# Stationary operands of the 512-column one-pass products: rounded part and rest stored apart, or element by element side by side

## The reference, cut to what matters

```python
def swiglu(h, w_gate, w_up, w_down):
    return (jax.nn.silu(h @ w_gate) * (h @ w_up)) @ w_down

for e in range(N_EXPERTS):                       # moe_swiglu
    y = swiglu(t, w_gate[e], w_up[e], w_down[e])
    out = out + combine[:, e:e + 1] * y.astype(jnp.float32)

def squared_relu_mlp(n, w1, w2):
    return jnp.square(jax.nn.relu(n @ w1)) @ w2
```

## Time and profile before

| what | value |
|---|---|
| three executions | 2759.27, 2763.17, 2770.59 us; median 2763.17 us |
| profiled execution, first to last instruction (span) | 2767.1 us |
| TensorE: matmuls (PE), weight loads (PEld) | 2704.7 us (98%), 2291.4 us (83%) |
| VectorE (DVE), ScalarE (ACT), GpSimd (POOL) | 1978.5 us (72%), 1665.1 us (60%), 86.5 us (3%) |
| HBM read, written | 697.28 MB, 18.87 MB: 259 GB/s over the span |
| mean granted TensorE clock | 0.990 |

### The profile page before, as it was taken

How to read it: one execution, slowest core, us unless ns; L and a number is a source line. 1 busy time by engine, 2 the same in 40 slices (tenths; PEclk the granted TensorE clock), 3 DMA queues, 4 the chain that set the end, 5 groups by cost and what they waited for, 6 DMA issues and landing times. The chain is left out here.

```text
span 2767.1 us, 38903 instructions
## 1 busy us (share of the span) xinstructions
PE 2704.7 (98%) x15424; PEld 2291.4 (83%) x15424; DVE 1978.5 (72%) x2069; ACT 1665.1 (60%) x1965; POOL 86.5 (3%) x86
## 2 busy tenths in 40 slices
PE   8999999999999999999999999999999999999998
PEld 5878999788988888888888888889768998867897
DVE  4756655586779998989899898986655555474555
ACT  3575444558467777777777777766445445354544
POOL 1000100110001000000000000011000000000000
PEclk8999999999999999999999999999999999999999
DMA  9847854865579999999999999986424544414452
GB/s 346 299 139 273 321 203 146 278 226 198 172 289 385 393 377 378 377 374 379 380 374 375 381 373 376 378 276 194 142 92 146 189 183 136 170 62 153 183 190 77
DMA packets 317754, 718.08 MB, mean 260 GB/s; under 512 B 7990, under 2 KB 26916, under 8 KB 317620
## 3 DMA queue, kind: packets, MB, share of 16 engines
q1 hardware_dynamic: 311488, 697.99, 69.5%
q0 software_dynamic: 5520, 18.02, 2.0%
q10 hardware_dynamic: 612, 0.18, 0.0%
HBM read 697.28 MB, written 18.87 MB: 259 GB/s over the span
## 5 line engine op out<-in xcount | busy, mean ns | idle before, releaser
L2775 DVE TENSOR_TENSOR ring_rest<-ring,weights_hi 128x2048 fp32r<-128x2048 f32 x270 | 607.5, 2284 | 9.7 <-ACT weights_hi L2100 7.3
L2100 ACT ACTIVATE weights_hi<-ring 128x2048 fp32r<-128x2048 f32 x270 | 516.6, 1916 | 131.9 <-PE ps L1833 75.7
L1831 PE MATMUL ps<-weights_hi,xg_hi 128*128 128x512 f32 x1008 | 400.9, 398 | 0.7 <-DVE xg_lo L2775 0.7
L1833 PE MATMUL ps<-weights_hi,xg_lo 128*128 128x512 f32 x1008 | 395.0, 392 | 0.0
L1832 PE MATMUL ps<-ring_rest,xg_hi 128*128 128x512 f32 x792 | 310.2, 392 | 0.0
L2100 ACT ACTIVATE arena<-ps 128x512 f32<-128x512 f32 (+6 forms) x307 | 157.3, 529 | 220.0 <-PE ps L1833 54.1
L1852 PE MATMUL ps<-weights_hi,hidden_split_moe 128*128 128x512 f32 x1008 | 284.1, 393 | 1.3 <-DVE hidden_split_moe L2775 1.1
L2775 DVE TENSOR_TENSOR w_split<-ring,w_split 128x1024 fp32r<-128x1024 f32 x128 | 150.9, 1221 | 154.5 <-ACT w_split L2100 154.5
L2775 DVE TENSOR_TENSOR ring_rest<-ring,mix_hi 128x2048 fp32r<-128x2048 f32 (+2 forms) x76 | 173.4, 2284 | 117.2 <-ACT mix_hi L2100 116.7
L2775 DVE TENSOR_TENSOR late_rest<-arena,weights_hi 128x2048 fp32r<-128x2048 f32 x108 | 244.5, 2286 | 5.3 <-ACT weights_hi L2100 4.3
L2100 ACT ACTIVATE weights_hi<-arena 128x2048 fp32r<-128x2048 f32 x108 | 207.0, 1917 | 62.3 <-PE ps L1833 32.5
(11 more groups left out here) (310 smaller groups left out, 5289.5 us busy)
## 6 DMA issues: line engine op xcount, KB each, us to landing
ring<-in_moe_w_gate_dram SPq DMA_DIRECT2D x54, 2048.0 KB, 10.1
ring<-in_moe_w_up_dram SPq DMA_DIRECT2D x45, 2048.0 KB, 10.1
ring<-in_moe_w_down_dram SPq DMA_DIRECT2D x36, 2048.0 KB, 9.2
ring<-in_mlp_w_dram SPq DMA_DIRECT2D x32, 2048.0 KB, 8.8
arena<-in_moe_w_down_dram SPq DMA_DIRECT2D x27, 2048.0 KB, 9.9
ring<-in_w_mod_dram SPq DMA_DIRECT2D x48, 1024.0 KB, 8.8
ring<-in_w_in_dram SPq DMA_DIRECT2D x48, 1024.0 KB, 6.2
arena<-in_moe_w_up_dram SPq DMA_DIRECT2D x18, 2048.0 KB, 10.4
```

Of the source, the lines that this page charges most:

```text
L1831: pe.matmul(b, xg_hi[:, k, :], hi[:, i, :], start=(k == 0), stop=False)
L1833: mm = pe.matmul(b, xg_lo[:, k, :], hi[:, i, :], start=False, stop=(k == KD - 1))
L2100: return act.activation(o, i, func, **kw)
L2775: return dve.tensor_tensor(o, a, b, op)
```

## The change

Each of the stationary tiles gets the part (rounded, rest) as its innermost dimension instead of an outer one. Element i of the rounded part and element i of the rest are then neighbours; a weight load reads 128 elements that are two elements (8 bytes) apart, and the ACT and DVE instructions that write a part write every second element. The sizes, the start addresses of the tiles, the instructions, their order and their waits stay as they are.

```diff
@@ -737,7 +737,7 @@
 
 
         expert = Region(xc_at, arena_cols - xc_at)
-        hidden_split_moe = rounded("hidden_split_moe", free_at + 2 * HALF_LINE, 2, 512)
+        hidden_split_moe = rounded("hidden_split_moe", free_at + 2 * HALF_LINE, 512, 2)
         xn_moe = expert.cut(TT, D)
         rows_moe = xn_moe[:, 0]
         to_slots = Region(rope1_at, TT * P).cut(TT, P)
@@ -761,8 +761,9 @@
         ring_rest = nc.alloc_sbuf_tensor_at("ring_rest", [P, RING_A, SLOT], F32R,
                                             offset=ring_offset)
         late_rest = rounded("late_rest", late_at, 2, SLOT)
-        xg_hi, xg_lo = rounded("xg_hi", TT * D, KD, P), rounded("xg_lo", TT * D + KD * P, KD, P)
-        xg = Region(TT * D + KD * P, KD * P).cut(KD, P)
+        xg_pairs = rounded("xg_pairs", TT * D, KD, P, 2)
+        xg_hi, xg_lo = xg_pairs[:, :, :, 0], xg_pairs[:, :, :, 1]
+        xg = Region(TT * D, 2 * KD * P).cut(KD, P, 2)[:, :, :, 1]
         before_me, all_ones = (Region(y_at + i * P, P).cut(P) for i in range(2))
         gain_row = Region(TT * D, D).cut(D)
         rpp = Region(y_at + 2 * TT * P, 512)
@@ -829,13 +830,13 @@
         hi_early_2 = rounded("hi_early_2", lru_at + 2 * TT * D, 2048)
         oT_hi = rounded("oT_hi", cross_at + 7744 + HALF_LINE, KD, T)
         hi_late_2 = rounded("hi_late_2", cross_at + 10240 + 2 * HALF_LINE, 2048)
-        hidden_split = rounded("hidden_split", cross_at + 8192 + 4 * HALF_LINE, 2, 4, 512)
+        hidden_split = rounded("hidden_split", cross_at + 8192 + 4 * HALF_LINE, 4, 512, 2)
 
         w_split_ffn = {"in": [rounded("w_in_ffn_0", lru_at + SLOT + HALF_LINE, 2, 2048), rounded("w_in_ffn_1", sg_at, 2, 2048)],
                        "out": [rounded("w_out_ffn_0", lru_at + SLOT, 2, 2048),
                                rounded("w_out_ffn_1", sg_at + 3 * HALF_LINE, 2, 2048)]}
         hT_hi_ffn = rounded("hT_hi_ffn", lru_at + TT * D, KD, T)
-        hidden_split_ffn = rounded("hidden_split_ffn", qT_at + 3 * HALF_LINE, 2, 4, T)
+        hidden_split_ffn = rounded("hidden_split_ffn", qT_at + 3 * HALF_LINE, 4, T, 2)
         setup2 = Region(pipe_at + 2816, 1280)
         posk_i, posq_i = setup2.cut(T).bitcast(I32), setup2.cut(TT).bitcast(I32)
         gain_row2 = Region(pipe_at + 2048, D).cut(D)
@@ -1751,7 +1752,7 @@
 
                             def out_part(t, c, m, q):
                                 sw, sx = parts[q]
-                                return pe.matmul(acc(t, c), hidden_split_ffn[:, sx, (2 * j + m) % 4, t * P:(t + 1) * P],
+                                return pe.matmul(acc(t, c), hidden_split_ffn[:, (2 * j + m) % 4, t * P:(t + 1) * P, sx],
                                                  w[:, sw, m, c * 512:(c + 1) * 512],
                                                  start=(j == 0 and m == 0 and q == 0),
                                                  stop=(j == FT // 2 - 1 and m == 1 and q == 2))
@@ -1849,7 +1850,7 @@
                         at = (2 * half + m) * P
                         for q, (w, sx) in enumerate([(hi, 0), (lo, 0), (hi, 1)]):
                             for c in range(2):
-                                mm = pe.matmul(acc(0, c), hidden_split_moe[:, sx, at:at + P],
+                                mm = pe.matmul(acc(0, c), hidden_split_moe[:, at:at + P, sx],
                                                w[:, m, c * 512:(c + 1) * 512],
                                                start=(g == 0 and half == 0 and m == 0 and q == 0),
                                                stop=(g == GROUPS - 1 and half == 1 and m == 1 and q == 2))
@@ -2058,7 +2059,7 @@
 
                         def out_part(t, c, m, q):
                             sw, sx = parts[q]
-                            return pe.matmul(acc(t, c), hidden_split[:, sx, j % 4, m * T + t * P:m * T + (t + 1) * P],
+                            return pe.matmul(acc(t, c), hidden_split[:, j % 4, m * T + t * P:m * T + (t + 1) * P, sx],
                                              w[:, sw, m, c * 512:(c + 1) * 512],
                                              start=(j == 0 and m == 0 and q == 0),
                                              stop=(j == n2 - 1 and m == 1 and q == 2))
@@ -2464,7 +2465,7 @@
                     act.wait_ge(emptied["dve"], plan.nth["ffn", j])
                     if j >= 4:
                         act.wait_ge(pe_done, value["ffn_out", (j - 4) // 2])
-                    f(hidden_split_ffn[:, 0, j % 4], hg[:, j % 4], ACT.Copy).then_inc(sem("ffn_hidden_rounded"), 1)
+                    f(hidden_split_ffn[:, j % 4, :, 0], hg[:, j % 4], ACT.Copy).then_inc(sem("ffn_hidden_rounded"), 1)
 
                 if l == 0:
                     round_weights(0)
@@ -2536,7 +2537,7 @@
                 else:
                     act.wait_ge(pe_done, step_at(lambda i: ("moe_down", i, GROUPS - 2), e, 1))
                     act.wait_ge(sem("hidden_moe_ready"), of_turn_at(GROUPS, GROUPS + 1, e, 1))
-                f(hidden_split_moe[:, 0, half * 256:half * 256 + 256], acc(1, 1)[:, half * 256:half * 256 + 256],
+                f(hidden_split_moe[:, half * 256:half * 256 + 256, 0], acc(1, 1)[:, half * 256:half * 256 + 256],
                   ACT.Copy).then_inc(sem("hidden_moe_rounded"), 1)
 
             def expert_head(e):
@@ -2553,7 +2554,7 @@
                             round_weights_of(p + HI_BUFFERS, e)
                     elif kind == "turn":
                         act.wait_ge(pe_done, step_at(lambda i: ("moe_T", i, at[0]), e))
-                        f(hidden_split_moe[:, 0, :], acc(1, 1), ACT.Copy).then_inc(sem("hidden_moe_rounded"), 1)
+                        f(hidden_split_moe[:, :, 0], acc(1, 1), ACT.Copy).then_inc(sem("hidden_moe_rounded"), 1)
                     else:
                         act.wait_ge(pe_done, step_at(lambda i: ("back", i), e))
                         f(to_tokens, acc(1, 0)[:, 0:T], ACT.Copy, accum_out=slot_weight)\
@@ -2732,7 +2733,7 @@
                     act.wait_ge(sem("squared"), n2 * l + j + 1)
                     if j >= 4:
                         act.wait_ge(pe_done, value["mlp_down", l, j - 4])
-                    f(hidden_split[:, 0, j % 4], squared[:, j % 2], ACT.Copy)\
+                    f(hidden_split[:, j % 4, :, 0], squared[:, j % 2], ACT.Copy)\
                         .then_inc(sem("hidden_rounded"), 1)
 
                 n2 = FF2 // P // 2
@@ -3197,7 +3198,7 @@
 
                 def rest_of_hidden(j):
                     dve.wait_ge(sem("ffn_hidden_rounded"), j + 1)
-                    tt(hidden_split_ffn[:, 1, j % 4], hg[:, j % 4], hidden_split_ffn[:, 0, j % 4].bitcast(F32),
+                    tt(hidden_split_ffn[:, j % 4, :, 1], hg[:, j % 4], hidden_split_ffn[:, j % 4, :, 0].bitcast(F32),
                        ALU.subtract).then_inc(sem("ffn_hidden_split_ready"), 1)
 
                 if l == 0:
@@ -3381,7 +3382,7 @@
             def rest_of_hidden(nth, a, z, e, back=0):
 
                 dve.wait_ge(sem("hidden_moe_rounded"), of_turn_at(nth, GROUPS + 1, e, back))
-                tt(hidden_split_moe[:, 1, a:z], acc(1, 1)[:, a:z], hidden_split_moe[:, 0, a:z].bitcast(F32),
+                tt(hidden_split_moe[:, a:z, 1], acc(1, 1)[:, a:z], hidden_split_moe[:, a:z, 0].bitcast(F32),
                    ALU.subtract).then_inc(sem("hidden_moe_ready"), 1)
 
             def outputs_taken(e):
@@ -3643,7 +3644,7 @@
 
                 def rest_of_hidden(j):
                     dve.wait_ge(sem("hidden_rounded"), n2 * l + j + 1)
-                    tt(hidden_split[:, 1, j % 4], squared[:, j % 2], hidden_split[:, 0, j % 4].bitcast(F32),
+                    tt(hidden_split[:, j % 4, :, 1], squared[:, j % 2], hidden_split[:, j % 4, :, 0].bitcast(F32),
                        ALU.subtract).then_inc(sem("hidden_split_ready"), 1)
 
                 n2 = FF2 // P // 2
```

## The result

| | before | after |
|---|---|---|
| median of the executions compared | 2762.24 us (2759.27 to 2770.59, n = 4) | 2793.26 us (2790.75 to 2795.99, n = 4) |
| span of the profiled execution | 2767.1 us | 2790.8 us |
| mean granted clock there | 0.990 | 0.993 |

The change makes the kernel **slower by 31 us**: ratio 1.0112, 95% interval 1.0094 to 1.0129. The forecast was 49.5 us faster. The measured time lies inside the stated range, which reached into the slower case, but on the other side of the time before.

The account below looks back on a forecast made before the run. TensorE's pace between products was taken as the bound. Saving 8.9 ns each gave experts 40.4, squared-ReLU 6.8 and SwiGLU 2.3 us, together 49.5 off 2763.2: 2713.7 us, range 2682 to 2805 (8 in 10).

Parts of the forecast that it names:

- the slower case: Every changed weight load disturbs the moving stream more: 14 to 86 us slower, up to 2849 us; chance 0.27.
- The test sentence: Distances above 0.2288 us between products with no wait between would prove the step from contiguous to paired reading wrong.
- a one-pass product that lies well against its load: 6.6 ns left of 15.5: Value chosen for the changed 512-column products' excess over column time: 8.9 ns saved each, 49.5 us in all.
- the two ends: Bounds on the strided weight load's effect over 5568 products: -81 us if excess nearly vanishes, +86 us if it doubles.
- can stay clear of each other: At step two the load moves through addresses as fast as the moving stream, so their distance stays and collisions may cease.
- comparison (b): 256-column products took 118.1 ns in layer 0, 113.3 in layer 1, same lines and tiles: excess 11.4 or 6.6 ns.
- all there is to win: The 15.5 ns each 512-column product takes over its columns' 213.3 ns; 86 us over 5568 products.
- Rival 2: Every changed weight load touches twice the memory pieces, each costing the moving stream: 15.5 ns more each, 2849 us; chance 0.27.
- L2052 and L1743 were to keep their distances: Expected sign in the timeline of weight loads: these products, like the unrounded ones, start as far apart as before.
- Rival 1: Nothing changes, 2763 us: excess comes from load timing, not addresses, or DMA stays at 375 to 384 GB/s; chance 0.18.
- The Trainium skill's rule: SBUF lines are 16 bytes; full rate needs two hits per line, and each crossing to a new line pays.

Follow-up runs that it names:

- pairs_written: Changed kernel's strided writes in experts and squared-ReLU, but weight loads read 128 neighbouring elements; SwiGLU as before the change: 2759.93 us, 0.9997 of the kernel before.
- pairs_read: Kernel before with contiguous writes, but expert and squared-ReLU weight loads take every second element of two neighbouring blocks: 2787.93 us, ratio 1.0093.
- Experiment 5: TensorE-only kernel of 48-product stretches, varying start and step of the stationary read: at start 48, 229.2 ns per product at step 1, 233.3 at step 2.
- aligned_experts: Kernel before with only the experts' two stationary tiles moved to start where their moving operands do, modulo 64 elements: 2755.27 us, ratio 0.9964.
- experiment 6: TensorE-only stretches with narrower stationary operands, finer starts, further steps, fewer moving columns: 128 to 32 stationary columns at start 0 took 227.3 to 233.2 ns.

## Why the prediction was wrong

**Right: the bound and the count.** TensorE's distance between starts is what the kernel is made of, 5568 products hang on the changed tiles, and nothing else of the change reaches the time: pairs_written puts the writes at nothing, pairs_read the reads at 26.5 us of the 31. The test sentence held: distances above 0.2288 us with no wait between them, so the step from contiguous to paired reading failed.

**Wrong: the step "a one-pass product that lies well against its load: 6.6 ns left of 15.5".** This is the value chosen between the two ends, -14.5 and +15.5 ns for each product. Measured: +4.1 to +4.6 ns. I took it because with a step of two the streams keep their distance and so "can stay clear of each other", while contiguous loads drift past the moving stream. By that picture a contiguous load shouldn't care where it starts, and with a step of two the starts 16 and 48, both an odd multiple of 16 elements, should be alike. Experiment 5 shows neither: step 1 goes from 227.3 to 233.5 ns with the start, and step 2 is 3.4 ns better than step 1 at start 16 and 4.1 ns worse at start 48. The direction was a matter of the start, which I had read off the code and used as if any odd multiple of 16 helped. No row of before could decide it, and the chances, 0.55 for faster against 0.27 for slower, didn't say so.

**Wrong: the reading of comparison (b).** I read 113.3 and 118.1 ns at equal addresses as a collision whose size depends on how the streams lie, and took the smaller for my forecast. But 6.6 ns was the excess of 256 columns. It was never shown that 512 columns can reach it: the best distance of 512 columns in any view shown is 226.6 ns (aligned_experts), an excess of 13.3, and 320 and 384 columns have 13.4 and 13.3 too in experiment 6. So of the 15.5 ns that I called all there is to win, 2.2 ns were to be had by the starts and steps that I tried, 12 us of 86.

**Rival 2 had the sign and not the mechanism.** It priced 15.5 ns for a doubling of the pieces touched. The runs exclude a price per piece: step 32 costs 233.8 ns, step 2 at start 16 less than step 1, a quarter of a load no less than a whole one. Its threshold of 2.5 ns was passed with 4.5, and 5568 x 4.5 ns = 25 us is most of the 31.

**What no case had.** L2052 and L1743 were to keep their distances. They didn't: some 6 us of the difference lie in 256-column products whose code wasn't touched and which stood at the slower of their two levels. Whether the change put them there is not shown: in SwiGLU they also stood there in two of five profiles of runs that left that stage as before (pairs_read, aligned_experts). The earlier trace rows had shown both levels; I used them as evidence and didn't ask what it costs if the change shifts them.

**A wrong sum.** Rival 1 has "9 to 24 us are gained at most" if DMA stays at 375 to 384 GB/s. At 384 a turn would take 375 x 119.6 / 384 = 116.8 us, so 9 x 2.8 = 25 us in the experts and 9 elsewhere, 34 in all. Nothing else was worked out from it.

**The Trainium skill's rule.** It stands in SBUF — State Buffer, section on the DMA port swizzle. Its half on two hits per line agrees with the load's own record (188 to 194 ns at step 2, which is two hits in a line of 16 bytes; 310 ns at step 4, which is one). Its half on crossings has the sign of this case, at start 48, and the wrong sign at start 16. The size that I worked out from it, 86 us, is nearly three times too large, and as a count of lines it fails: steps 4, 12 and 32 all cross into 128 lines and gave 239.7, 270.0 and 233.8 ns.

**What stays open.** Why the distances are what they are and why they repeat after 64 elements; why step 2 with both tiles at 48 isn't what it is with both at 0; what moves a stretch from one level to the other. Shown are that the read and not the write costs, that the distance depends on step and start, its period over the starts tried, and that TensorE alone reproduces both kernels' distances.

## What to carry to other kernels

In a kernel that TensorE bounds with one-pass products and a weight load beside each, the start of the stationary slice against the moving one is a parameter worth up to 3% of each product (226.6 to 233.5 ns): measure the distance at four starts, in a kernel of a few stretches, before and after any change of layout. At the best start of each a contiguous read was the cheaper one (227.0 against 230.1 ns), so keep stationary reads contiguous and choose their start; a strided write to a tile cost nothing here, where its writer isn't late, so where two layouts are wanted let the write carry the step. When a gain shows in the touched products and not in the time, list the distances of the untouched ones too.

## What the runs showed of the hardware that I had not expected

- The distance of a 512-column fp32r product with a load beside it depends on the start modulo 64 elements: 227.3, 233.5, 232.3, 229.2 ns at 0, 16, 32, 48 with contiguous loads.
- A load at step 2 keeps nearly its pace (194 ns), at step 4 its record is 310 ns, and the product's distance then still is only 238.6 to 239.9 ns.
- A step of 2 on the moving operand doubles the product: 453 ns instead of 230.
- With 320 and 384 moving columns at start 48 the step of two costs nothing (146.8 and 146.7, 173.3 and 173.6 ns).
- Stretches of 256 columns stand at 113.3 or 117.8 ns, stretches of 512 at 227.2 or 229.6, and can change from one repetition to the next with nothing changed in the code.
- ScalarE's write with a step of two took 665 ns for 512 elements instead of 620, VectorE's 689 instead of 683.
